# Whole-row sums for the first modulation, additions shared by VectorE and GpSimd, and a later place for the second up group's weights

## The reference, cut to what matters

```python
h = rmsnorm(x, norm_pre_mix) * (1 + scale_m) + shift_m
y = token_mixer(h, ...)                     # windowed attention, delta rule, gates, four projections
x = x + gate_m * rmsnorm(y, norm_post_mix)
h = rmsnorm(x, norm_pre_ffn) * (1 + scale_f) + shift_f
y = peer_ffn(h, ...)                        # top 16 of 16384 experts per head, down, gelu, up
out = x + gate_f * rmsnorm(y, norm_post_ffn)
```

## Time and profile before

| what | value |
|---|---|
| time, median of 3 runs | 5153.44 us (5152.69 to 5156.43) |
| profiled execution, its own time | 5148.03 us |
| its span | 5146.2 us |
| TensorE clock granted, mean | 0.984 of full |

### The profile page before, as it was taken

The page is one execution under the profiler, slowest core; times in us unless marked ns, Lnnn a source line. Parts: engine busy times, 40 slices in busy tenths (PEclk is TensorE's granted clock), DMA queues, the critical chain, the costliest instruction groups (busy, mean ns, idle before and its releaser), DMA issues.

```text
span 5146.2 us, 65300 instructions
## 1 busy us (share of the span) xinstructions
PE 4962.2 (96%) x24570; PEld 4265.0 (83%) x24570; DVE 2360.9 (46%) x5125; ACT 1646.3 (32%) x2183; POOL 2684.2 (52%) x1356
## 2 busy tenths in 40 slices
PE   4899999999999999899899999999999999999997
PEld 2688887888888888788588888888888899999997
DVE  6333203434444433554666799400000266676764
ACT  3222222444444442222322222222222333333332
POOL 2333333222222223334244488888885688888872
PEclk7999999999999999999999999999999999999999
DMA  9322223222222225666333333333333588888983
GB/s 308 107 86 89 81 90 143 89 88 93 95 93 98 90 94 197 246 245 245 114 112 108 119 120 121 119 122 123 120 121 133 207 301 313 318 315 312 330 316 125
DMA packets 253833, 841.97 MB, mean 164 GB/s; under 512 B 37713, under 2 KB 86993, under 8 KB 215025
## 3 DMA queue, kind: packets, MB, share of 16 engines
q1 hardware_dynamic: 140432, 562.09, 31.7%
q10 hardware_dynamic: 78432, 143.55, 7.9%
q0 software_dynamic: 34816, 134.52, 7.0%
HBM read 766.91 MB, written 71.57 MB: 163 GB/s over the span
## 4 chain that ended last, share of the span: by engine, by line
PE 58%; issue 31%; POOL 6%; DMA 3%; DVE 2%; ACT 0%; POOLq 0%; ACTq 0%; SPq 0%; DVEq 0%
PE bank L878 10%; PE bank L880 10%; PE bank L882 10%; PE bank L944 7%; PE bank L946 7%; PE bank L945 7%; POOL lo L483 6%; PE bank L561 2%; PE bank L563 2%; PE bank L565 2%; DMA half<-ada_late 2%; PE wide L575 0%; DMA R<-xT 0%; DVE R L1872 0%; POOL R L479 0%
## 5 line engine op out<-in xcount | busy, mean ns | idle before, releaser
L483 POOL TENSOR_TENSOR lo<-raw,hi 128x2048 fp32r<-128x2048 f32 x168 | 772.1, 4596 | 1622.6 <-ACT hi L1003 1622.6
L489 POOL TENSOR_TENSOR lo<-raw,hi 128x1024 fp32r<-128x1024 f32 x528 | 1270.4, 2407 | 592.8 <-ACT hi L1310 587.0
L561 PE MATMUL bank<-xh,hi 128*128 128x512 f32 x2336 | 977.4, 418 | 16.8 <-POOL lo L483 9.1
L1310 ACT ACTIVATE hi<-raw 128x1024 fp32r<-128x1024 f32 x528 | 547.8, 1057 | 1259.1 <-PE bank L882 1089.6
L565 PE MATMUL bank<-xh,lo 128*128 128x512 f32 x2336 | 916.1, 392 | 0.0
L563 PE MATMUL bank<-xl,hi 128*128 128x512 f32 x2336 | 913.7, 391 | 0.0
L878 PE MATMUL bank<-xh,hi 128*128 128x512 f32 x2176 | 850.5, 391 | 8.7 <-DVE xl L1553 8.6
L880 PE MATMUL bank<-xl,hi 128*128 128x512 f32 x2176 | 847.5, 389 | 0.0
L882 PE MATMUL bank<-xh,lo 128*128 128x512 f32 x2176 | 847.4, 389 | 0.0
L944 PE MATMUL bank<-CH,hi 128*128 128x384 f32 x2048 | 693.3, 339 | 10.3 <-DVE R L2049 6.5
L946 PE MATMUL bank<-CH,lo 128*128 128x384 f32 x2048 | 687.5, 336 | 0.0
(11 more groups left out here) (312 smaller groups left out, 6333.2 us busy)
## 6 DMA issues: line engine op xcount, KB each, us to landing
raw<-stream SPq DMA_DIRECT2D x528, 512.0 KB, 3.6
raw<-stream SPq DMA_DIRECT2D x168, 1024.0 KB, 4.8
half<-ada_late SPq DMA_DIRECT2D x128, 512.0 KB, 4.4
arow<-stream SPq DMA_DIRECT2D x64, 512.0 KB, 6.2
act_d<-etile ACTq DMA_DIRECT2D x128, 256.0 KB, 2.0
G_d<-dn_zero ACTq DMA_DIRECT2D x16, 1536.0 KB, 6.7
Gt<-G_d ACTq DMA_DIRECT2D x32, 768.0 KB, 11.1
cf<-act_d ACTq DMA_DIRECT2D x31, 768.0 KB, 17.0
```

Source lines behind the costliest of these rows:

```text
L483: nc.gpsimd.tensor_tensor(lo[s][:, :], raw[s][:, :], hi[s][:, :].bitcast(F32), ALU.subtract).then_inc(raw_used[s], 1)
L489: nc.gpsimd.tensor_tensor(lo_h[slot], raw_h[h % 4], hi_h[slot].bitcast(F32), ALU.subtract).then_inc(f_lo[h % 4], 1)
L561: nc.tensor.matmul(out, hi[slot][:, w], at_k(x[0], k), start=(k == 0), stop=False, skip_group_check=True)
L1310: nc.scalar.activation(hi_h[slot], raw_h[h % 4], ACT.Copy).then_inc(f_hi, 1)
```

## The change

Four edits:

1. *First sums over whole rows.* The 32 rows of 8 KB a partition are loaded whole (1 MB each) through four slots, the two `raw` buffers and the two `hi` buffers. VectorE sums 16 rows for the shift and then 16 for the scale in `acc`, in SBUF. TensorE adds over the partitions after each 16, VectorE adds the bias. Then `modulated(0, 0, ...)`, the form of the feed-forward stage, runs over all 16 slices (GpSimd's multiplications go), ScalarE makes the high parts of units 0 and 1 after slices 6 and 10, and units 0 and 1 are plain calls of `product`, with the small weights' products between their steps. The row transposes move from unit 3, step 5 to unit 2, step 1. The first two units' loads come behind the 32 rows.
2. *Stage behind the mixer.* The root stays in PSUM (bank 6). In even slices VectorE only multiplies, and GpSimd adds x; in odd slices VectorE's product goes to PSUM and VectorE adds. GpSimd's eight additions stand ahead of its low halves.
3. *Second up group.* In the first group the weightings of the next one stand behind additions 8, 9, 11 and 12 (before: 1, 4, 7, 10), the low parts behind 10, 11, 13 and 14; on ScalarE the high halves of the next group's first weights go ahead of the coefficients' high parts.
4. *Output.* As in 2, with bank 0 for the root and GpSimd adding in the even slices.

The diff, cut to its core (what else it has are the counts of `raw_used` and `s_adamm` that shift, and the removed `load_ada`, `add_rows`, `first_gains`, `first_low` and `first_products`, which stand above):

```diff
+        acc = place("acc", [P, D], F32, r2)
...
+        arow = raw + [place(f"arow{s}", [P, D], F32, offset[f"hi{s}"]) for s in range(2)]
...
+        arow_full = raw_full + [sem(f"arow_full{s}") for s in range(2)]
+        arow_used = raw_used + [sem(f"arow_used{s}") for s in range(2)]
...
 
@@ -412,24 +409,15 @@
                     sp.wait_ge(half_used[n % 2], n // 2 - 1)
                 sp.dma_start(late_slot(n), ada_late[n, :, :]).then_inc(half_full[n % 2], 16)
 
-            def load_ada(n):
-
-                q, m = divmod(n, KT // 2)
-                if n >= 2:
-                    sp.wait_ge(arow_full[n % 2], n // 2 * 32)
-                if n >= 4:
-                    sp.wait_ge(arow_used[n % 2], n // 2 - 1 + ONE)
-                for e in range(2):
-                    both = stream[0:U_ADA, :, q * QN:(q + 1) * QN].rearrange("(v k) p n -> p k v n", v=2)
-                    sp.dma_start(arow[n % 4][:, e * 2 * QN:(e + 1) * 2 * QN].rearrange("p (v n) -> p v n", v=2),
-                                 both[:, 2 * m + e, :, :]).then_inc(arow_full[n % 2], 16)
-
+            with sp.Fori(0, ADA_USES) as i:
+                for s in range(4):
+                    sp.wait_ge(arow_used[s], i + ONE)
+                    sp.dma_start(arow[s][:, :], stream[bass.ds(i * 4 + s, 1), :, :].rearrange("a p n -> (a p) n")
+                                 ).then_inc(arow_full[s], 16)
             for s in range(2):
-                load(0, s)
-            for n in range(ADA_LOADS):
-                load_ada(n)
+                load(ADA_USES, s)
...
             for k in range(KT):
-                sp.wait_ge(s_out, k + 1)
+                if k % 2:
+                    sp.wait_ge(s_out, k // 2 + 1)
+                else:
+                    sp.wait_ge(s_x2p, KT // 2 + k // 2 + 1)
                 sp.dma_start(outT[k * P:(k + 1) * P, :], R1[:, k, :]).then_inc(s_stored, 16)
...
         def _(pool):
-            pool.wait_ge(s_rs, 1)
-            for k in range(KT):
-                nc.gpsimd.tensor_tensor(R1[:, k, :], R1[:, k, :], rs[:, :], ALU.mult).then_inc(s_h, 1)
...
+            for k in range(0, KT, 2):
+                pool.wait_ge(s_x2, KT + k // 2 + 1)
+                nc.gpsimd.tensor_tensor(R1[:, k, :], R1[:, k, :], x2b[:, k, :], ALU.add).then_inc(s_x2p, 1)
...
-            def first_products(k):
-
...
-            for q in range(QUARTERS):
-                pe.wait_ge(s_hs, q + 1)
-                if q:
-                    pe.wait_ge(s_ada, q)
-                for n in range(2 * QT):
-                    mm = nc.tensor.matmul(bank[3][:, n:n + 1], acc[:, n * P:(n + 1) * P], ones[:, 0:1],
...
+            with pe.Fori(0, 2) as c:
+                pe.wait_ge(arow_used[3], (c + 1) * (KT // 4) + ONE)
+                for n in range(KT):
+                    mm = nc.tensor.matmul(bank[0][:, n:n + 1], acc[:, n * P:(n + 1) * P], ones[:, 0:1],
                                           start=True, stop=True, skip_group_check=True)
                 mm.then_inc(s_adamm, 1)
-                for k in range(q * QT, (q + 1) * QT):
-                    first_products(k)
+                pe.wait_ge(s_ada, c + 1)
 
             def rows_between(u, k):
-                if u == 3 and k == 5:
+                if u == 0 and k == 0:
+                    pe.wait_ge(s_in, 64)
+                if u == 0 and k or u == 1 and k == 0:
+                    r = u * KT + k - 1
+                    pe.wait_ge(s_lo, r + 1)
+                    nc.tensor.matmul(bank[2][0:48, :], wba_h[:, r, :], at_k(xh, r), start=(r == 0), stop=False,
+                                     skip_group_check=True)
+                    nc.tensor.matmul(bank[2][0:48, :], wba_h[:, r, :], at_k(xl, r), start=False, stop=False,
+                                     skip_group_check=True)
+                    mm = nc.tensor.matmul(bank[2][0:48, :], wba_l[:, r, :], at_k(xh, r), start=False,
+                                          stop=(r == KT - 1), skip_group_check=True)
+                    if r == KT - 1:
+                        mm.then_inc(s_ba, 1)
+                if u == 2 and k == 1:
                     pe.wait_ge(s_row, 1)
                     for c in range(TT):
                         mm = nc.tensor.transpose(bank4[3][:, c, 0:48], cc(row[1], c), cst[0:48, C_ID:C_ID + 48])
...
+                    product(u % 2, u // 2, bank[u % 2][:, :], attention_between(h, a),
+                            ready=None if u else (s_lo, 0))
...
-                root = out if n == 2 else rs
+                root = bank[6] if n == 1 else out
...
-            for s in range(2):
...
-            for q in range(QUARTERS):
-                act.wait_ge(arow_used[1], (q + 1) * (KT // 4) + ONE)
-                if q:
-                    act.wait_ge(s_adamm, q + ONE)
-                nc.scalar.activation(acc[:, :], hacc[0], ACT.Copy).then_inc(s_hs, 1)
...
+            for k in range(KT):
+                act.wait_ge(s_h, k + 1)
+                shifted(k, xh, part(SHIFT_M), s_hi)
+                if k in (6, 10):
+                    s = (k - 6) // 4
+                    act.wait_ge(arow_used[2 + s], ADA_USES + ONE)
+                    high(s, 0)
...
             for k in range(KT):
-                act.wait_ge(s_x2, k + 1)
+                if k % 2:
+                    act.wait_ge(s_x2, k + 1)
+                else:
+                    act.wait_ge(s_x2p, k // 2 + 1)
                 act.wait_ge(s_ss, 2 * KT + k - 1)
                 nc.scalar.activation(sq[k % 2][:, :], R1[:, k, :], ACT.Square).then_inc(s_sq, 1)
                 if k % 3 == 2 and k < 12:
...
                 if m == 0:
                     take_activations(1, 0)
                     take_activations(1, 1)
+                    for c in range(FOUR):
+                        ups_ahead(1, 0, c)
                 coefficient_high(m + 1, 0)
                 take_activations(m + 1, 2)
                 coefficient_high(m + 1, 1)
                 take_activations(m + 1, 3)
                 coefficient_high(m + 1, 2)
                 for c in range(2):
-                    ups_ahead(m + 1, 0, c)
+                    if m:
+                        ups_ahead(m + 1, 0, c)
                 coefficient_high(m + 1, 3)
                 for c in range(2, FOUR):
-                    ups_ahead(m + 1, 0, c)
+                    if m:
+                        ups_ahead(m + 1, 0, c)
...
+            with dve.Fori(0, 2) as c:
+                for k in range(KT):
+                    s = k % 4
+                    dve.wait_ge(arow_full[s], (c * (KT // 4) + (k // 4 + 1)) * 16)
+                    if k == 0:
+                        dve.wait_ge(s_adamm, c + ONE)
+                        v.tensor_scalar(acc[:, :], arow[0][:, :], cond[:, 0:1], None, ALU.mult
+                                        ).then_inc(arow_used[0], 1)
+                    else:
+
+                        dve.wait_ge(arow_used[(k - 1) % 4], c * (KT // 4) + ((k - 1) // 4 + 1) + ONE)
+                        v.scalar_tensor_tensor(acc[:, :], arow[s][:, :], cond[:, k:k + 1], acc[:, :],
+                                               ALU.mult, ALU.add).then_inc(arow_used[s], 1)
+                dve.wait_ge(s_adamm, c + 1 + ONE)
+                v.tensor_tensor(ada[:, bass.ds(c * KT, KT)], bank[0][:, 0:KT], vec[:, bass.ds(c * KT + V_BADA, KT)],
+                                ALU.add).then_inc(s_ada, 1)
...
-            for n in range(ADA_LOADS):
-                add_rows(n)
-                q, m = divmod(n, KT // 2)
-                if q and m == 1:
-                    first_gains(q - 1)
-                if q and 2 <= m < 2 + QT:
-                    first_low((q - 1) * QT + m - 2)
-            first_gains(QUARTERS - 1)
-            for k in range(KT - QT, KT):
-                first_low(k)
+            dve.wait_ge(s_ada, 2)
+            gains(0, SCALE_M)
+            step.sync()
...
+            modulated(0, 0, R1, part(SHIFT_M))
...
             for k in range(KT):
-                step(v.scalar_tensor_tensor(mixed[:, k, :], mixed[:, k, :], coef[:, 1, k:k + 1], rs[:, :],
-                                            ALU.mult, ALU.mult))
-                step.sync()
-                v.tensor_tensor(R1[:, k, :], xin[:, k, :], mixed[:, k, :], ALU.add).then_inc(s_x2, 1)
+                y = bank[4 + k // 2 % 2][:, :] if k % 2 else mixed[:, k, :]
+                if k % 2 and k >= 5:
+                    dve.wait_ge(s_x2, k - 3)
+                ins = v.scalar_tensor_tensor(y, mixed[:, k, :], coef[:, 1, k:k + 1], bank[6][:, :], ALU.mult, ALU.mult)
+                if k % 2:
+                    step(ins)
+                    step.sync()
+                    ins = v.tensor_tensor(R1[:, k, :], xin[:, k, :], y, ALU.add)
+                ins.then_inc(s_x2, 1)
             modulated(2, 2, R1, part(SHIFT_F))
...
                     add(m, n)
-                    if m + 1 < UPS and n in (1, 4, 7, 10):
-                        weighted(m + 1, n // 3)
```

(21 more changed lines are left out.)

105 lines of the change are left out of this document (21 added, 84 removed).

## The result

The changed kernel takes 5119.93 us (median of 4 runs, 5119.35 to 5121.55), beside 5153.06 us for the kernel before on the same chip (4 runs, 5149.45 to 5156.43). The ratio is 0.9936, 95% interval 0.9919 to 0.9954: faster, by 33.1 us. The prediction was 5120.3 us. The total came out almost exactly, in part by luck: two of its four terms were too large, by about as much as the profiled execution of before lay under its median.

The account below looks back on a forecast made before the run. TensorE, busy 96% of the span, was the bound; gains count only where it stands still. 5.7 + 13.6 + 8.4 + 5.4 = 33.1 us off the profiled 5148.0, plus 5.4 to the median: 5120.3 us, range 5110 to 5138.

Parts of the forecast that it names:

- The start, 5.7 us: First sums over whole rows: sums end at 109.2, unit 3 starts at 179.2, 5.7 us gained.
- the stop of some 4 us: Start, between the two passes of sums: a pause of some 4 us, mostly hidden by four slots, 1 us added.
- The 4.0 us from the last sum to the first slice: Start: from the sums' end at 109.2 to the first scaled slice at 113.2, 4.0 us.
- The moved wait: Row transposes now in unit 2: TensorE stands there for 3.6 us.
- Behind the mixer, 13.6 us: Stage behind the mixer: VectorE's 30.4 us become 16.4, less 0.4 of lag; 13.6 us gained, bounds 8.6 and 14.0.
- I take 0.4 ... most of the lag is made up before the last slice: Stage behind the mixer: TensorE's sums of squares start slowly but cost only 0.4 us of the gain.
- Rival 4: Norm stage: TensorE stays at the lower clock, 1.36 a tile, 5 us less gain, 5125; chance 0.07, within the forecast's.
- rival 3: Stage behind the mixer and output: GpSimd still holds VectorE, 1.27 us a pair, total 5141; chance 0.10.
- The up group, 8.4 us: Second up group: later weightings remove TensorE's wait at the first group's additions, 8.4 us gained, low bound 5.
- Rivals 1, 2 and 5: Start: sums slightly late, 5129 to 5134 (0.16); whole rows at 290 GB/s, 5149 (0.06); transfers and sums alternating, 5194 (0.03).
- rival 6: Up group: the hole stays in another place, total 5129; chance 0.05.
- The output, 5.4 us: Final stage: VectorE's 22.3 us become 16.4, less half a microsecond for the last stores; 5.4 us gained, bounds 0 and 5.9.

## Why the prediction was right, and where it wasn't

- **The start, 5.7 us.** Measured 4.5 at unit 3 (184.54 + 0.4 - 180.45), 4.3 to 6.6 at the later landmarks of two profiles, and 8.8 in the medians. The middle of this is near the term, but two of its sizes were off in opposite directions. The rate was 423 GB/s, not 388, which put sums and transfers level (2.35 us a sum, 2.37 forecast; 2.45 from one to the next). And "the stop of some 4 us" was 7.7: the sum over the partitions is now of 16 columns in place of 8, 32 records in 6.98 us. The 4.0 us from the last sum to the first slice were carried over from the earlier trace rows, where there were half as many columns; they measured 7.9. The sums ended at 108.05 (109.2 forecast), the first slice was at 115.99 (113.2). That counts only stretches where TensorE stands still was not right here either: the gain came as shorter busy time.
- **The moved wait**, 3.6 us, measured 2.36. What the prediction left out is the clock behind it: in six of thirteen profiles it fell there, for 1.7 or 3.1 us more (last section). With it the start would have given 1.4 to 1.7 us up to `yl` in place of 4.8.
- **Behind the mixer, 13.6 us.** Measured 10.7. VectorE's 16.4 us was right to 0.1. What failed is the step "I take 0.4 ... most of the lag is made up before the last slice". The last sum of squares ended 3.2 us further behind VectorE than before. With VectorE faster, ScalarE and TensorE set the pace at some 1.12 us a slice, so little is made up; 1.9 of the 3.2 is the lower clock (1.2 GHz) at the beginning, which the run with TensorE kept busy took away. Rival 4 described this part, at a bound of 5 us.
- **GpSimd's hold** (rival 3) was rightly set low: with one PSUM operand there is none (0.69 and 0.75 us beside GpSimd). Even with the root in SBUF it would have been 0.29 us a pair, not 1.27.
- **The up group, 8.4 us.** 8.5 by the landmarks of the two kernels, 7.5 to 10.0 by undoing it. Right, with its working.
- **The rivals on the rate and on the hole.** Rivals 1, 2 and 5 fell with 414 to 423 GB/s and 2.45 us a row, rival 6 with copies 2.09 us apart.
- **The output, 5.4 us.** VectorE's 16.4 was right, but the profiles gave 3.3 (5.1 by the medians of the run that undoes it). The step left out what follows the last store: GpSimd, which had long been done before, now ends the program with its drain, 4.8 us behind its last addition.
- **The sum.** Against the profiled execution, 33.1 was forecast and 28.5 came: 3 too few behind the mixer and 2 at the output, while the stretches up to the mixer gave half a microsecond more than the start's term. Against the median 33.1 came. The 5.4 us that I added for the distance between that execution and the median turned out to belong to the kernel before alone; after has its profiled run 0.5 us from its median. That the total was hit to 0.4 us is luck: those two errors cancelled.

## What to carry to other kernels

When an engine that set the pace gets faster, work out the pace of the next two in the chain before booking its whole gain, and look at what clock TensorE will have after waiting for it. Give work to an idle engine only until that engine's own end becomes the last thing: here nearly half of VectorE's gain at the output was lost to it in the profile, and seven additions in place of eight were faster. Before sharing an operation between VectorE and GpSimd, try to move one operand into PSUM; that alone gave three to four fifths of what the stage gained.

## What the runs showed of the hardware that I had not expected

- GpSimd's drain at the program's end took 6.05 us from the start of its last addition in each of the eleven kernels that end so, and ended 4.8 us behind that addition. In the three that end with low halves its record is 11.4 us long, but it too ended 4.7 us behind the last low half.
- TensorE needs 6.98 us for 16 products with a single column each (32 records) at the granted clock 0.50, 0.22 us a record.
- 2 KB runs against whole 8 KB rows cost 423 to 387 GB/s, at a share of the DMA engines of 1.05 and 1.01. At 290 GB/s the kernel before had the share 0.97, so the share doesn't tell how fast a transfer could be.
- What the clock does behind the wait in unit 2 is not the same in every execution. TensorE waits 2.35 or 2.36 us ahead of the transposes in all thirteen profiles of kernels that have it there. In the 7 us behind it the granted clock was 1.00 in seven of them, 0.76 in two and 0.52 to 0.53 in four, and from the transposes to `yl` it was 489.3 to 489.4, 491.0 and 492.4 to 492.5 us. Windows of after, then of the kernel with the root in SBUF, whose code is the same up to there:

```profile
171.00:175.00 4.00, 4.00 (x18) 3.24 (x18) 2.16 (x5) 2.52 (x2) 1.14 (x1) 1.00 0.14 33
```

```profile
171.00:175.00 4.00, 4.00 (x13) 3.14 (x12) 2.16 (x5) 2.51 (x2) 0.83 (x1) 0.50 0.14 33
```

This is what puts `yl` near 660 us in some executions and near 663 in others. What decides it isn't shown, and neither is how often it comes in runs without a profile.
